# Splitting and reordering the VectorE, ScalarE and GpSimd steps of a seven-stage transformer kernel in full precision

## The chip, the cores and the metric

One core of a Trainium2 chip runs one kernel. The metric is device time in microseconds (us), the median of repeated executions. The engines are PE (TensorE, matmuls), DVE (VectorE), ACT (ScalarE), POOL (GpSimd) and SP (SyncE, which issues weight DMAs). Each has its own instruction stream and runs it in order; semaphores order the engines among each other.

## The reference, cut to what matters

Two blocks are computed on 512 tokens of width 1024, in float32 accuracy.

```python
# first_block, DEPTH = 2
for layer in range(2):
    f = swiglu(rms_norm(h, g[0]), gate[layer, 0], up[layer, 0], down[layer, 0]); h = h + 0.5 * rms_norm(f, g[1])
    hm = rms_norm(h, g[2])
    mix = pool_mixer(hm, ...) if layer == 0 else dilated_mixer(hm, cos, sin, w_q, k_sh, v_sh, w_o)
    h = h + rms_norm(mix, g[3])
    f = swiglu(rms_norm(h, g[4]), gate[layer, 1], up[layer, 1], down[layer, 1]); h = h + 0.5 * rms_norm(f, g[5])
# pool_mixer: u = hm @ w_in; p = causal means over 2, 4, 8, 16 tokens (one width per group of 256) - u;
#             ((p @ w_group) * scale) @ w_out
# dilated_mixer: rope(q), rope(k), three dilated windows, 8 heads of 64 each; softmax over the windows' log sums; @ w_o
# second_block, 2 layers, with 256 context tokens beside the 512
h = x * (1 + scale) + shift
q, k, v, gates ... = split(h @ w_in)          # also for the context tokens
y = [hgrn2 scan both ways, dense attention with rope, differential attention with rope, window attention with sink]
x = layer_norm(alpha * x + gate * ((y * silu(g)) @ w_out))
```

## The kernel before

Activations are kept feature-major: `hc` holds 8 blocks (`KC`) of 128 features by up to 768 tokens (`TOK`, 512 and 256 of context). Float32 accuracy comes from splitting each operand in two parts of fewer bits and making three matmuls per block: high x high, low x high and high x low (`mm3`, L1320). A weight tile is 128 by 1024. It is loaded by SP into `raw` (four slots); ACT copies it to its high part `wh` (L944), POOL subtracts to get the low part `wl` (L843, L855), and then PE may use it. The low part of the activations, `xl` or `al`, comes from DVE (`x_low`, L1973) or POOL (L893, L910).

The stages follow each other: a feed-forward (ffn) of layer 0 (0 to 395 us), the pool mixer (395 to 635, into which the next ffn's start falls), two ffns (the second, ffn(1,0), from 935), dilated attention (1335 to 1735), the fourth ffn (to 2131), and then the two layers of the second block (2131 to 2945 and 2945 to 3630), here called the last two layers. At each boundary `add_f` (L1977) normalizes the stage's result on DVE, adds it to `hc` block by block and makes the next stage's `xl`.

**Pool.** `POOL_TILES` (L48) is the order of ten weight tiles: eight "in" tiles, each followed by the means on DVE (L2114 to L2128), a high copy on ACT (L1058) and a low part on POOL (L910); and two "group" tiles on PE (L1495), which use PSUM banks 4 to 7.

**Rope tables.** `rope_tables` (L2142) computes angles on DVE at the start of ffn(1,0), and ACT makes two sines of them (L1027), in the same stream in which it copies `wh`.

**Dilated attention.** `dilated_steps` (L282) writes the order of PE, DVE and ACT: q, k and v tiles are computed in four quarters, after which "finish" adds a rotation matmul on PE (L1546), and at given quarters an "event" computes a unit of scores (L1560 the scores, L1566 the mask). DVE prepares rotated q and k (L2170, L2186). `kv_low` (L2220) makes the low parts of the normalized input of k and v. The output projection (L1641) begins when all low parts of the attention result are there (L1938), and DVE takes two PSUM banks at a time.

**The last two layers.** `mixer_steps` (L380) writes one list of steps per layer. Each engine walks through the same list and does its own share of every step, so the list sets the order within each engine. The steps are:

- `quarter` (a quarter of a 24-matmul weight tile on PE; with part 3, ACT's `wh` and gating of a tile and POOL's `wl`), `finish` (after a tile: rotations and splits on DVE, L2395 to L2444), `table` (ACT's DMA of a rope table);
- `scores` and `exps` of an attention (scores by query rows, whose maximum and sum give the softmax's row constants; ACT L1227), `rows` (DVE and ACT math of these constants, L2487 to L2513, transposed by PE, L1799, and copied by ACT, L1241);
- `weights` (scores again, by key, PE L1788, L1815; exponents by ACT L1250), `values` (PE L1836, L1846, L1879), `end` (normalization on DVE);
- steps of the two-way scan, the "ticks" of `scan_ticks`: `sums` in three stages (DVE L2308 to L2344, ACT L1154 the closing exponent), `dist` (POOL L876), `products` (PE L1681 to L1686, DVE L2267 to L2289), `step` (PE L1698 to L1709), `update` (L2304).

The waits between the engines are semaphores on each of these results.

## Time and profile before

| | us |
|---|---|
| median of 3 runs | 3629.45 (3626.37 to 3630.61) |
| profiled execution, own time | 3632.27 |
| span of that execution | 3630.3 |
| last two layers (2131 to 3630.3) | 1499.3 |

The span is the time between the first and the last instruction. Busy times of one engine are sums of its instructions; they can overlap those of the other engines, and matmuls overlap their neighbours on PE. The figure that says most is the idle time in front of an instruction and the work that ended it: "PE ps L1799 <- DVE work L2513" is PE at line 1799 waiting for what line 2513 wrote. "issue" says that no work of another engine ended the idle time. PEclk is the clock that TensorE was granted, 1.00 being 2.4 GHz.

### The profile page before, as it was taken

How to read it: one execution, taken by the hardware profiler on the slowest of the kernel's cores; microseconds unless marked ns; L12 is line 12 of the kernel's file. 1: busy time of each engine (PE TensorE's matmuls, PEld its weight loads, DVE VectorE, ACT ScalarE, POOL GpSimd, SP SyncE). 2: the span in 40 equal slices, each digit the busy share in tenths (PEclk: the TensorE clock that was granted, in tenths of full speed). 3: DMA queues.
4: the chain of work that ended last, by engine and by line, in shares of the span. 5: the costliest groups of instructions: out<-in, count | busy, mean ns of one | idle time of the engine just before them, and what ended most of it. 6: DMA issues, size and time to landing. Idle time of an engine off the chain costs nothing.

```text
span 3630.3 us, 53848 instructions
## 1 busy us (share of the span) xinstructions
PE 3244.4 (89%) x20644; PEld 2434.3 (67%) x20644; DVE 1747.4 (48%) x3135; ACT 1146.8 (32%) x1963; POOL 1216.3 (34%) x998
## 2 busy tenths in 40 slices
PE   7999889999899998998899988788979878688787
PEld 5888668777678776776678766555756655455454
DVE  4343765334634364444524366553653266554534
ACT  3222333212422132112312233443434234444343
POOL 3444444444344432222344444311331233213211
PEclk9999999999999999999999989988989988898889
DMA  3222222433233321111233321000101111001011
GB/s 134 93 98 97 77 82 82 139 122 110 100 126 107 133 81 64 53 59 47 81 133 110 122 105 36 25 19 24 36 14 64 47 53 36 30 25 36 24 53 41
DMA packets 74356, 264.66 MB, mean 73 GB/s; under 512 B 7856, under 2 KB 9136, under 8 KB 73904
## 3 DMA queue, kind: packets, MB, share of 16 engines
q1 hardware_dynamic: 67104, 242.25, 19.4%
q10 hardware_dynamic: 7056, 19.69, 1.5%
q8 instruction: 137, 2.24, 0.3%
q14 instruction: 59, 0.48, 0.0%
HBM read 252.47 MB, written 7.34 MB: 72 GB/s over the span
## 4 chain that ended last, share of the span: by engine, by line
PE 71%; DVE 15%; issue 7%; ACT 4%; POOL 2%; DMA 0%; ACTq 0%; DVEq 0%; POOLq 0%
PE ps L1320 53%; PE ps L1815 2%; PE ps L1836 2%; PE ps L1788 2%; POOL wl L855 1%; PE ps L1398 1%; DVE work L2071 1%; DVE tb L2473 1%; PE ps L1681 1%; DVE tb L2118 1%; PE ps L1623 1%; PE ps L1379 1%; PE ps L1641 1%; DVE hc L1984 1%; PE ps L1701 1%
## 5 line engine op out<-in xcount | busy, mean ns | idle before, releaser
L855 POOL TENSOR_TENSOR wl<-raw,wh 128x1024 fp32r<-128x1024 f32 x320 | 791.8, 2474 | 1220.6 <-ACT wh L966 705.4
L1320 PE MATMUL ps<-xh,wh 128*128 128x512 f32 x2400 | 916.2, 406 | 97.5 <-POOL wl L843 30.9
L1320 PE MATMUL ps<-xl,wh 128*128 128x512 f32 x2400 | 864.5, 385 | 0.0
L1320 PE MATMUL ps<-xh,wl 128*128 128x512 f32 x2400 | 862.8, 384 | 0.0
L1320 PEld LDWEIGHTS ps<-xh,wh 128*128 128x128 f32 x2400 | 442.8, 196 | 277.9 <-issue 155.5
L966 ACT ACTIVATE wh<-raw 128x1024 fp32r<-128x1024 f32 x224 | 237.6, 1061 | 982.4 <-PE ps L1320 934.0
L843 POOL TENSOR_TENSOR wl<-raw,wh 128x1024 fp32r<-128x1024 f32 x90 | 220.3, 2448 | 918.0 <-ACT wh L944 918.0
L1320 PEld LDWEIGHTS ps<-xl,wh 128*128 128x128 f32 x2400 | 443.1, 196 | 93.3 <-issue 13.1
L1320 PEld LDWEIGHTS ps<-xh,wl 128*128 128x128 f32 x2400 | 441.2, 195 | 87.6
L1320 PE MATMUL ps<-ah,wh 128*128 128x512 f32 x1104 | 437.5, 403 | 25.4 <-issue 14.2
L1320 PE MATMUL ps<-al,wh 128*128 128x512 f32 x1104 | 420.5, 388 | 0.0
L1320 PE MATMUL ps<-ah,wl 128*128 128x512 f32 x1104 | 420.3, 388 | 0.0
L944 ACT ACTIVATE wh<-raw 128x1024 fp32r<-128x1024 f32 x186 | 196.4, 1057 | 546.9 <-PE ps L1320 496.7
L1227 ACT ACTIVATE tb<-tb,work 128x256 f32<-128x256 f32 (+2 forms) x288 | 165.8, 576 | 385.0 <-DVE work L2479 185.8
L1320 PEld LDWEIGHTS ps<-ah,wh 128*128 128x128 f32 x1104 | 205.6, 189 | 106.6 <-issue 51.2
L2473 DVE TENSOR_SCALAR_CACHE_REDUCE tb<-ps 128x256 f32<-128x256 f32 (+2 forms) x288 | 135.3, 518 | 262.1 <-PE ps L1788 192.8
L2071 DVE TENSOR_TENSOR work<-work 128x512 f32<-128x512 f32 x88 | 245.2, 2786 | 0.0
L1320 PEld LDWEIGHTS ps<-ah,wl 128*128 128x128 f32 x1104 | 205.4, 189 | 43.1
L1320 PEld LDWEIGHTS ps<-al,wh 128*128 128x128 f32 x1104 | 206.0, 190 | 40.2 <-issue 2.0
L2067 DVE TENSOR_TENSOR work<-ps,rs 128x512 f32<-128x512 f32 x66 | 45.7, 692 | 300.2 <-PE ps L1320 300.1
L876 POOL TENSOR_TENSOR hc<-hc 128x64 f32<-128x64 f32 x280 | 95.7, 342 | 169.2 <-PE ps L1686 145.1
L1836 PE MATMUL ps<-work 128*64 128x512 f32 (+2 forms) x448 | 124.3, 636 | 21.0 <-issue 14.1
(348 smaller groups left out, 3625.3 us busy)
## 6 DMA issues: line engine op xcount, KB each, us to landing
raw<-wts_dram SPq DMA_DIRECT2D x458, 512.0 KB, 3.4
spilled_dram<-hc ACTq DMA_DIRECT2D x1, 3072.0 KB, 8.7
hc<-spilled_dram ACTq DMA_DIRECT2D x1, 3072.0 KB, 12.8
tb<-tab_dram ACTq DMA_DIRECT2D x5, 512.0 KB, 3.7
hc<-x_dram ACTq DMA_DIRECT2D x8, 256.0 KB, 9.2
spilled_dram<-hc ACTq DMA_DIRECT2D x1, 2048.0 KB, 7.2
hc<-spilled_dram ACTq DMA_DIRECT2D x1, 2048.0 KB, 9.3
out_dram<-hc SPq DMA_DIRECT2D x8, 256.0 KB, 2.1
```

What stands on the lines that cost most here:

```text
L843: pool.tensor_tensor(wl[:, n % SPLIT, :], raw[:, LOADED[n] % RAW, :], wh[:, n % SPLIT, :].bitcast(F32), ALU.subtract).then_inc(lo_done, 1)
L855: pool.tensor_tensor(wl[:, n % SPLIT, :], raw[:, LOADED[n] % RAW, :], wh[:, n % SPLIT, :].bitcast(F32), ALU.subtract).then_inc(lo_done, 1)
L876: pool.tensor_tensor(z[way], border, k_, ALU.subtract)
L944: act.activation(wh[:, n % SPLIT, :], raw[:, at % RAW, :], ACT.Copy).then_inc(hi_done, 1)
L966: act.activation(wh[:, n % SPLIT, :], raw[:, at % RAW, :], ACT.Copy).then_inc(hi_done, 1)
L1227: ins = act.activation(b, b, ACT.Exp, bias=m[:, lane, t:t + 1], scale=scale, accum_out=d[:, lane, t:t + 1])
L1320: ins = pe.matmul(out_, w[:, s, k * P:(k + 1) * P], x_(k, at), start=first, stop=last)
L1788: ins = pe.matmul(ps[:, score_bank(a) + lane, col_:col_ + n], x_[r0:r0 + w, q_tile * P:(q_tile + 1) * P], y_[r0:r0 + w, tok:tok + n], star ...
L1815: ins = pe.matmul(outs[lane], stat, mov, start=number == 0, stop=number == 3 and not g["masks"], skip_group_check=True)
L1836: pe.matmul(flat[HEAD * h:HEAD * (h + 1), g["q0"]:g["q0"] + g["n"]], vv, pring[t % len(pring)][:, 0:g["n"]], start=g["first"], stop=g["las ...
L2071: dve.tensor_tensor(tt[:, j, :], tt[:, j, :], sil[:, j, :], ALU.mult).then_inc(dve_own, 1)
L2473: ins = dve.tensor_scalar(scores_copy[:, lane, col_:col_ + n], ps[:, score_bank(a) + lane, col_:col_ + n], 1.0, -3e38, ALU.mult, ALU.max, ...
```

## The change

1. `add_f`: `xl` of block k-1 is made before the addition of block k, not after it.
2. Pool: the group-2 tile moves behind the last two in tiles; the two groups get banks of their own (`group_bank`, `pool_bank`), so that PE waits for fewer PSUM banks to come free (the second group no longer waits for the first one's four low parts, and the output tiles run in other banks); POOL makes the `wl` of the next tile before the `al` of the tile ahead.
3. `rope_tables` on DVE moves from the start of ffn(1,0) to the start of ffn(0,1), in buffers that are free there. ACT's sines stay.
4. Dilated: the scores' event of a v tile moves from quarter 1 to quarter 2, so that two products of three matmuls stand between the rotation and the scores that need it; `kv_low` is spread in three pieces; the output projection begins with three of four blocks before it waits for the last low part, and DVE takes one bank at a time.
5. `mixer_steps`: ACT's and POOL's share of a finished tile becomes a step of its own, "round", which is put off behind the next `weights` (`later`); the second half of a rotation becomes "rope"; the row constants' math becomes "math", directly behind the last scores, and "rows" comes after the last `values`; "square" (ACT, differential attention) comes right behind the last `values`; "y", the split of a mixed result, moves from `end` of one attention to behind the first `values` of the next; DVE's wait for the rope table ("table_in") moves from the DMA's issue to before its first use; the scan's `sums` get up to six stages and extra ticks; a unit of scores is put in directly behind `values` where two or more are due.

In the diff, "..." marks what is left out.

```diff
-POOL_TILES = [("in", 6), ("in", 7), ("in", 4), ("in", 5), ("in", 2), ("in", 3), ("group", 2), ("in", 0), ("in", 1), ("group", 0)]
+POOL_TILES = [("in", 6), ("in", 7), ("in", 4), ("in", 5), ("in", 2), ("in", 3), ("in", 0), ("in", 1), ("group", 2), ("group", 0)]
...
+        if part == 3 or part == 1 and what != "v" or part == 2 and what == "v":
             event()
...
-        ticks += [[("sums", w, stage)] for stage in range(3)]
+        long = [["scan"], ["rest", "keys"]] if way else [["scan", "keys"]]
+        stages = [["abs"], ["logs"], *([["more"]] if layer else []), *long, ["exp"]]
+        ticks += [[("sums", w, stage) for stage in together] for together in stages]
+        ticks[-2].append(("dist", w, 0))
...
-    steps, ends, ticks = [], [], []
+    steps, ends, ropes, rounds, maths, ticks = [], [], [], [], [], []
 
     def scores(a, u):
+        if u == 0:
+            flush(ropes)
         steps.extend([("scores", a, u), ("exps", a, u)])
-
-    def quarter(f, part):
-        while f[0] == "g" and f[1] in SCANS and part == 3 and ("sums", 4 * layer + 2 * SCANS.index(f[1]) + 1, 0) not in steps:
+        if a and u == units[a] - 1:
+            maths.append(("math", a))
...
+    def flush(what):
+        steps.extend(what)
+        what.clear()
+
+    def quarter(f, part, later=False):
...
+        if part == 3:
+            flush(ropes)
+            flush(rounds)
+            if f in (("q", 2), ("q", 4)):
+                steps.append(("table_in",))
         steps.append(("quarter", f, part))
+        if part == 3:
+            rounds.append(("round", f))
+            if not later:
+                flush(rounds)
         if part == 3 and (f[1] not in SCANS and f[0] not in "gm" or f[0] == "i"):
             ends.append(("finish", f))
         if part == 3 and f in (("f", "s0"), ("f", "s1")):
             ticks.extend(scan_ticks(layer, SCANS.index(f[1])))
 
     def finishes():
-        steps.extend(ends)
+        if ends:
+            flush(rounds)
+        for _, f in ends:
+            steps.append(("finish", f))
+            if f[0] in "qk":
+                ropes.append(("rope", f))
         ends.clear()
...
+    def extra_tick():
+        if ticks and ticks[0][0][0] == "sums":
+            tick()
...
+            if i == 0:
+                finishes()
             if i + 1 < n:
                 steps.append(("weights", a, i + 1))
+            flush(rounds)
             finishes()
+            flush(maths)
             if i == n - 1 and not last:
                 for q in fill[i]:
                     quarter(*q)
                 finishes()
-                steps.append(("rows", a + 1))
                 fill[i] = []
             steps.append(("values", a, i))
+            if i == n - 1:
+                steps.append(("square", a))
+            if i == 0 and a:
+                steps.append(("y", a - 1))
+            extra_tick()
+            if len(due[i]) > 1:
+                scores(a + 1, due[i].pop(0))
             between = [None] if len(fill[i]) < 2 else [fill[i].pop(0), None]
             between += [*fill[i][:1], None, *fill[i][1:]]
             for number, step in enumerate(between):
                 if step:
-                    quarter(*step)
+                    quarter(*step, later=True)
                 else:
+                    flush(maths)
                     tick()
+                    flush(ropes)
                 if number % 2 == 0 and due[i]:
                     scores(a + 1, due[i].pop(0))
             for u in due[i]:
                 scores(a + 1, u)
+        flush(ropes)
+        if not last:
+            steps.append(("rows", a + 1))
         if a in (1, 3):
             finishes()
             tick(len(ticks))
+        quarter(*tail, later=True)
         if not last:
             steps.append(("weights", a + 1, 0))
-        quarter(*tail)
+        flush(rounds)
         steps.append(("end", a))
         if a == 3:
             steps.append(("reload",))
     finishes()
+    steps.append(("y", len(ATTENDS) - 1))
...
+        def group_bank(g0, b):
+            return (4 if g0 else 0) + b
+
+        def pool_bank(m):
+            return (m + 4) % 8
...
-                    elif step == "quarter" and at[1] == 3:
+                    elif step == "round":
                         remainder(c.at("tile"))
                         c.take("tile")
...
+                    late = []
                     for what, m in POOL_TILES:
                         remainder(c.at("tile"))
                         c.take("tile")
-                        if what == "in":
+                        for k in late:
                             pool.wait_ge(part_hi, c.take("part") + 1)
-                            pool.tensor_tensor(alk(m), tt[:, m % 2, :], ahk(m).bitcast(F32), ALU.subtract).then_inc(a_ready, 1)
-                        else:
-                            c.take("part", 4)
+                            pool.tensor_tensor(alk(k), tt[:, k % 2, :], ahk(k).bitcast(F32), ALU.subtract).then_inc(a_ready, 1)
+                        late = [m] if what == "in" else []
+                    c.take("part", 8)
...
-                wait_a(A_HEADS // 2)
+                wait_a(A_HEADS // 2 - 1)
                 settle()
+                c.take("a")
...
-                    ins.then_inc(tile_done, 1)
+                    for b, k in [(b, k) for k in range(4) for b in range(2)] if m == 0 else [(b, k) for b in range(2) for k in range(4)]:
+                        if (m, b, k) == (0, 0, 3):
+                            pe.wait_ge(a_ready, c.at("a"))
+                        blk = b * 4 + k
+                        for w, x_, first, last in ((wh, ah, k == 0, False), (wh, al, False, False), (wl, ah, False, k == 3)):
+                            ins = pe.matmul(ps[:, bb[b], :], w[:, n % SPLIT, blk * P:(blk + 1) * P],
+                                            x_[:, (KC + k) * SEQ:(KC + k + 1) * SEQ], start=first, stop=last)
+                        if k == 3:
+                            ins.then_inc(tile_done if b else half_full, 1)
...
                     own(dve.scalar_tensor_tensor(t, fo[:, k, :], gain(k), r, ALU.mult, ALU.mult))
+                    if k and name != "ada":
+                        x_low(k - 1, gain_of(name, *at))
                     give(dve.tensor_tensor(hc[:, k, 0:SEQ], hc[:, k, 0:SEQ], t, ALU.add), h_ready, "h")
                     if name == "ada":
                         modulated(at[0], k)
-                    elif k:
-                        x_low(k - 1, gain_of(name, *at))
...
-                ang, u, v = (fo[:, k, :] for k in range(3))
-                own(dve.tensor_copy(fo[:, 3, :], t1[:, 1, :].bitcast(I32)))
-                own(dve.tensor_scalar(ang, fo[:, 3, :], const("invf"), None, ALU.mult))
+                u, ang = t1[:, 0, :], t1[:, 1, :]
+                own(dve.tensor_copy(u, t1[:, 1, :].bitcast(I32)))
+                own(dve.tensor_scalar(ang, u, const("invf"), None, ALU.mult))
...
-                    give(dve.tensor_scalar(fo[:, 4 + s, :], v, PI_IN, -PI_IN, ALU.min, ALU.max), d2a, "d2a")
+                    give(dve.tensor_scalar(v, v, PI_IN, -PI_IN, ALU.min, ALU.max), d2a, "d2a")
...
                     if step == "quarter" and at[1] == 3:
                         take(*at[0])
                         if at[0] == DILATED_TILES[1]:
-                            kv_low()
+                            kv_low(0, 1, 2)
+                        if at[0] == DILATED_TILES[2]:
+                            kv_low(5, 6, 7)
                     elif step == "finish":
                         finish(*at)
+                        if at[0] == DILATED_TILES[1]:
+                            kv_low(3, 4)
...
                     if m:
-                        add_square(m - 2), add_square(m - 1)
+                        add_square(m - 1)
+                    b = 2 * (c.at("tile") % 2)
+                    dve.wait_ge(half_full, m // 2 + 1)
+                    dve.tensor_copy(fo[:, m, :], ps[:, b, :]).then_inc(half_taken, 1)
+                    dve.wait_ge(half_taken, m // 2 + 1)
+                    add_square(m)
                     n = tile()
-                    b = 2 * (n % 2)
-                    took(dve.tensor_copy(fo[:, m:m + 2, :], ps[:, b:b + 2, :]), n)
-                add_square(KC - 2), add_square(KC - 1)
+                    took(dve.tensor_copy(fo[:, m + 1, :], ps[:, b + 1, :]), n)
+                add_square(KC - 1)
                 add_f(norm_gain(1, 3), "ffn", 1, 1)
```

How the rows move on the engines, at three places:

PE, dilated attention, first k tile with a unit of scores (L1546/L1609 is the rotation, L1560/L1623 the scores, L1320/L1385 quarters of the v tile). Before:

```order
L1546 MATMUL ps<-work,cn 128x512
L1560 MATMUL ps<-work 128x128 x8
L1566 MATMUL ps<-mk 128x128 x8
L1320 MATMUL ps<-ah,wh 128x512
L1320 MATMUL ps<-al,wh 128x512
```

Changed:

```order
L1609 MATMUL ps<-work,cn 128x512
L1385 MATMUL ps<-ah,wh 128x512
L1385 MATMUL ps<-al,wh 128x512
L1385 MATMUL ps<-ah,wl 128x512
L1385 MATMUL ps<-ah,wh 128x512
L1385 MATMUL ps<-al,wh 128x512
L1385 MATMUL ps<-ah,wl 128x512
L1623 MATMUL ps<-work 128x128 x8
L1629 MATMUL ps<-mk 128x128 x8
```

Six matmuls now stand between the rotation and the scores.

DVE, layer 0 of the last two, around the row constants of the third attention (L2440 to L2444 is the end of a rotation, L2495 to L2513 the row constants; L2523 to L2527 and L2578 to L2596 in the changed kernel). Before:

```order
L2341 MEMSET work 128x256
L2342 MEMSET hc 128x128
L2440 TENSOR_TENSOR work<-work,tb 128x512
L2441 TENSOR_TENSOR work<-work 128x512
L2442 CAST ex<-work 128x512
L2444 TENSOR_TENSOR ex<-work,ex 128x512
L2495 TENSOR_TENSOR work<-work 128x16
L2502 TENSOR_TENSOR work<-work 128x16
```

Changed:

```order
L2556 TENSOR_SCALAR tb,work<-ps 128x256 x4
L2570 TENSOR_SCALAR work<-work 128x2x2
L2578 TENSOR_TENSOR work<-work 128x16
L2585 TENSOR_TENSOR work<-work 128x16
L2586 TENSOR_TENSOR work<-work 128x16
L2590 TENSOR_TENSOR work<-work 128x24
```

The row constants follow their last scores (L2556, L2570), and the rotation comes behind them.

ACT, the last layer, at the scan's sums (L1154/L1214 is their closing exponent, L1250/L1311 the exponents of the attention weights, L944/L1008 a `wh`, L1218/L1276 the rope table). Before:

```order
L1227 ACTIVATE tb,work<-tb,work 128x256 x4
L989 ACTIVATE hc<-hc 128x768
L990 ACTIVATE hc<-hc,sm 128x768
L1218 DMA tb<-tab_dram 128x1024
L1154 ACTIVATE work<-work,sm 128x768
L1250 ACTIVATE work<-ps 128x512 x2
```

Changed:

```order
L1285 ACTIVATE tb,work<-tb,work 128x256 x4
L1053 ACTIVATE hc<-hc 128x768
L1054 ACTIVATE hc<-hc,sm 128x768
L1276 DMA tb<-tab_dram 128x1024
L1311 ACTIVATE work<-ps 128x512 x2
L1008 ACTIVATE wh<-raw 128x1024
```

The weights' exponents and a `wh` no longer stand behind the closing exponent of the sums.

## Rows read from the trace of the kernel before

**Rows 1.** The page, part 1: busy us (share of the span) xinstructions

```profile
PE 3244.4 (89%) x20644; PEld 2434.3 (67%) x20644; DVE 1747.4 (48%) x3135; ACT 1146.8 (32%) x1963; POOL 1216.3 (34%) x998
```

**Rows 2.** Busy time by stretch: its length, PE, PEld, DVE, ACT, POOL busy, PEclk, DMA, GB/s

```profile
395.00:635.00 240.00, 216.14 (x863) 165.77 (x862) 149.25 (x161) 80.53 (x108) 97.46 (x43) 0.96 0.22 76
1335.00:1735.00 400.00, 362.56 (x2162) 270.58 (x2161) 183.22 (x224) 85.58 (x116) 99.44 (x40) 0.96 0.16 54
2131.00:2945.00 814.00, 677.10 (x6554) 486.51 (x6555) 422.30 (x1164) 315.61 (x695) 211.85 (x385) 0.90 0.10 36
2945.00:3630.30 685.30, 550.93 (x4588) 366.71 (x4588) 360.68 (x948) 279.23 (x597) 170.74 (x269) 0.87 0.11 38
```

**Rows 3.** PE's waits, 2131 to 3630.3: us in total, times, longest us

```profile
PE ps L1788 <- ACT work L1250: 39.2, 13, 15.7
PE ps L1799 <- DVE work L2513: 30.8, 10, 8.8
...
PE ps L1698 <- DVE work L2289: 24.0, 17, 6.9
...
PE ps L1815 <- issue: 17.6, 9, 4.9
...
PE ps L1815 <- ACT work L1250: 9.9, 5, 5.4
...
PE ps L1846 <- ACT work L1258: 8.9, 4, 3.3
```

**Rows 4.** Boundary: PE's waits 0 to 2131, and the timeline of DVE (start, us)

```profile
PE ps L1320 <- DVE xl L1975: 24.5, 5, 5.3
...
537.23 0.69 DVE L1984 TENSOR_TENSOR hc<-hc,work 128x512 f32<-128x512 f32 x1
```

**Rows 5.** Pool stage: PE's waits 395 to 635, then timelines of DVE and POOL

```profile
PE ps L1320 <- POOL wl L843: 6.1, 5, 2.9
PE ps L1495 <- POOL al L910: 4.3, 1, 4.3
...
473.53 0.67 DVE L2125 SCALAR_TENSOR_TENSOR work<-tb 128x496 f32<-128x496 f32 x1
...
477.25 2.72 DVE L2125 SCALAR_TENSOR_TENSOR work<-tb 128x496 f32<-128x496 f32 x1
...
475.37 1.30 POOL L910 TENSOR_TENSOR al<-work,ah 128x512 fp32r<-128x512 f32 x1 [2.42 <-ACT ah L1058]
476.64 2.81 POOL L843 TENSOR_TENSOR wl<-raw,wh 128x1024 fp32r<-128x1024 f32 x1
```

**Rows 6.** Rope tables: timelines of DVE, ACT and PE; DVE at ffn(0,1)'s start

```profile
949.53 0.42 DVE L2146 CAST work<-tb 128x512 f32<-128x512 int32 x1
...
959.03 0.63 ACT L1027 ACTIVATE tb<-work 128x512 f32<-128x512 f32 x1 [3.39 <-DVE work L2156]
...
963.07 0.80 PE L1320 MATMUL ps<-xh,wh 128*128 128x512 f32 x1 [7.07 <-POOL wl L855]
...
558.29 0.69 DVE L2065 TENSOR_TENSOR work<-ps,rs 128x512 f32<-128x512 f32 x1 [5.80 <-ACT rs L982]
```

**Rows 7.** Dilated attention: PE's waits, 1335 to 1735; one third of the output projection's matmuls

```profile
PE ps L1560 <- DVE work L2186: 11.1, 6, 1.9
PE ps L1546 <- DVE work L2170: 6.8, 5, 4.2
...
PE ps L1641 <- DVE al L1938: 4.0, 1, 4.0
...
L1641 PE MATMUL ps<-ah,wh x32: 388/389/796, 1701.8 to 1725.8; 128*128 128x512 f32 x32
```

**Rows 8.** Last layer: timelines of DVE and of ACT

```profile
3112.77 0.96 DVE L2325 SCALAR_TENSOR_TENSOR hc<-hc 128x768 f32<-128x768 f32 x1 [4.59 <-DMA tb<-tab_dram]
...
3120.26 0.93 ACT L1154 ACTIVATE work<-work,sm 128x768 f32<-128x768 f32 x1 [10.24 <-DVEq L2344]
```

**Rows 9.** POOL's waits, 2131 to 3630.3

```profile
POOL wl L843 <- ACT wh L944: 869.4, 74, 37.6
```

132 lines of the change are left out of this document (73 added, 59 removed).

## Prediction

> **What bounds the kernel now.** I read the page's first part, then busy time by stretch, then PE's waits, and last the timelines around the longest of them. PE is busy 89% of the span and no other engine is above half [rows 1], so what counts is PE's idle time and the clock PE is granted. In the last two layers PE is busy 677.1 of 814.0 us and 550.9 of 685.3 [rows 2]: 136.9 + 134.4 = 271.3 us idle, most of the kernel's idle 386 us (3630.3 - 3244.4). The granted clock there is 0.90 and 0.87, against 0.96 in the pool and dilated stages [rows 2]; at most 0.10 x 677.1 + 0.13 x 550.9 = 139 us of busy time is there because the clock was low. Two things can be won: idle time, and with it some of these 139 us, since PE's lower clock goes with the stretches that have more idle time. DVE is busy 52% of the time in these layers [rows 2], so it is no bound by volume; PE waits for it because of the order of its instructions.
>
> **The change, part by part.** Each term is a gain against the profiled execution, 3632.27 us, which stands 2.8 above the median of the runs.
>
> *Boundaries.* PE's first matmul of a stage waits for `xl`, 24.5 us in 5 places [rows 4]. At each, the addition of the next block, 0.69 us [rows 4], moves behind the `xl` that PE waits for. 5 x 0.69 = 3.5; I take **3**. Bounds: 1 (the last `xl` sets the end and nothing is won elsewhere) and 4.
>
> *Pool.* The removable waits are 6.1 us for `wl` in five places, and 4.3 for the `al` before the first group tile [rows 5]. With both group tiles last, that `al` is older, and `wl` ahead of `al` helps the first wait. Against it: the `wl` took 2.81 us directly behind an `al` of 1.30 [rows 5]; now this pair always runs as a block of 4.1 us, in which a DVE operation of 0.67 us took 2.72 [rows 5], and DVE sets the period of the means. I take half of 10.4, **5**, bounds -2 (2.72 - 0.67 once more than now) and 8. That a DVE operation on two SBUF inputs slows down beside POOL is stated in the Trainium skill, GPSIMD Engine Reference, in the table at its top: the SBUF interfaces are shared with VectorE. By that rule alone the amount of slowed work would stay, whichever of `wl` and `al` goes first, and this term would be nearly 0 instead of 5. The trace agrees with the rule in kind (0.67 against 2.72 us).
>
> *Rope tables.* PE stands 7.07 us at the first down tile of ffn(1,0) [rows 6]: ACT's second sine waits for DVE (3.39) and the `wh` for which POOL's `wl` is needed stands behind it. With the angles made one ffn earlier the sines wait for nothing: **about 8.5** (7.07 and some slow clock after it). But 9.5 us of DVE work, from its first row at 949.53 to the second sine at 959.03, now stand in front of the first multiplication of ffn(0,1), where DVE idles 5.80 us waiting for ACT's reciprocal root [rows 6]. The 3.7 us above that can make PE wait once; I charge 2.5. Net **6**, bounds 0 (the whole 7 returns there) and 8.
>
> *Dilated attention.* PE waits 11.1 us at the scores (6 long ones, up to 1.9) and 6.8 at rotations, 4.2 of it behind `kv_low`'s eight in a row; 4.0 before the output projection [rows 7]. The 96 matmuls of the output projection, in three groups of 32 like the one shown, take 24.5 us from first to last start [rows 7], 0.25 each; six are 1.5 us of cover for six waits of 1.85 in the mean: 9, and 1 of the other waits at rotations. Five of eight `kv_low` leave the spot: 3. Eighteen matmuls (4.6 us) before the last low part: 3. One bank instead of two as the last copy: 2. That is 18 of the 37.4 us idle in this stretch; its low clock costs at most 0.04 x 362.6 = 14.5, and 18/37.4 of that is 7. Together **25**. Bounds: 12 (half of the waits only move on, since DVE has the same work) and 35.
>
> *The last two layers, idle time.* By class [rows 3]:
> - L1788 behind ACT L1250, 39.2 in 13, one of 15.7: ACT's closing exponent of the scan sums waited 10.24 us for DVE, which itself waited 4.59 for the rope table [rows 8], and the weights' exponents queued behind it. The new order has these exponents ahead of the closing one: 15. The other 23.5: 10, from scores issued sooner and rounds (1.04 us of `wh`) put behind exponents.
> - L1799 behind the row constants L2513, 30.8 in 10: the math moves up before the rotation, and the last `values` lie between it and the transposes: 22; 9 is left, where DVE is late anyhow.
> - L1815, 17.6 and 9.9: PE at the weights with nothing or ACT to wait for: 12, as `wh` and gating no longer precede its exponents.
> - L1846 behind the square, 8.9: the square is now issued right after `values`: 6.
> - L1698 behind the scan's DVE chain, 24.0 in 17: 5, since DVE has as much to do as before.
>
> That is 70. What is put off has to be waited for somewhere: 55 rounds, the rope multiplications and "y". I charge 10. Net **60** of 271.3.
>
> *The clock.* 60/271.3 x 139 = 31; since 139 is an upper bound (the mean counts idle stretches too), **22**. Bounds for the two together: 25 (only the 15.7 and the squares go, 5 of clock) and 160 (39.2 + 30.8 + 17.6 + 9.9 + 8.9 = 106 idle, and 106/271.3 of 139, 54, for the clock).
>
> Where I could go wrong in reading rows 2 as work: the Trainium skill, Perfetto Trace Analysis (Identifying the Most-Contended Engine), holds that matmul busy time is a bad measure and the busy share of weight loads a better one. Here that is 486.5/814 = 60% and 366.7/685.3 = 54%, against PE's 83% and 80% [rows 2]. By it more than my 271 us could be won in these layers; the sum goes by idle time and clock.
>
> Sum: 3 + 5 + 6 + 25 + 60 + 22 = 121. 3632.3 - 121 = 3511; less 2.8 for the median (3508.5): **3508 us**.
>
> **The rivals.**
>
> *A, waits only move.* DVE has the same instructions in the last two layers (12 more rows in all); its chain (L1698) becomes what PE waits for next. Against it: DVE idles half the time. Then the last two layers give 25 and the other parts half of their terms or less, 1 + 1 + 2 + 15: 44, and the time is 3632 - 44 - 3 = 3585.
>
> *B, the clock comes back.* If a PE that idles less keeps 2.4 GHz in most stretches, clock and idle time give 80 + 60 instead of 82: 3632 - 39 - 140 - 3 = 3450. For it: with idle shares of 10 and 9% the pool and dilated stretches have 0.96, with 17 and 20% the last layers 0.90 and 0.87 [rows 2].
>
> *C, slower: late weights.* 55 of 76 rounds are put off behind weights' exponents. A round is 1.04 us of `wh` on ACT and then 2.4 to 2.8 of `wl` on POOL, 3.5 in all. If the tile's low part is late by this every time, PE stands 55 x 3.5 = 192 us and the time is 3508 + 192 = 3700. It decides from 121/55 = 2.2 us per round on. Against it: POOL waits for `wh` 869.4 us in 74 places, 11.7 each [rows 9], so `wl` is not short of POOL's time, and no wait of PE for L843 is among those of rows 3, whose view goes down to some 4 us. What the rows don't show is how early the tile is ready; that is why C keeps a chance.
>
> *D, the change does nothing measurable*: its steps are ordered otherwise but each wait is ended by the same data, 3629. The long waits of rows 3 and 8 are waits for order, not data, so this is unlikely.
>
> **How the numbers follow.** Forecast 0.66 (3470 to 3555), A 0.17, B 0.10, C 0.04, D 0.03. The range 3450 to 3590 holds the forecast, A's 3585 and B's 3450, and leaves out C, D and the ends beyond. A measurement of this kernel can tell about 0.2% (7 us) from no change. Faster by more than that: 0.66 + 0.17 + 0.10 = 0.93; same 0.03; slower 0.04.
>
> **What would show it.** Right: PE's wait at the first down tile of ffn(1,0) under 2 us; the scores' waits in dilated attention under 0.6 each; no wait above 10 us in the last two layers; L1799's successor waiting for DVE at most 10 us in all; idle there near 211 instead of 271 us, with PEclk 0.91 to 0.93 in the higher of the two. Wrong: PE waits for `wl` (L843's successor) in the last two layers (C); waits for DVE chains growing by what the others lost (A); PEclk unchanged while idle falls, which would make the clock term 0 and the time 3530.

## The result, and the profile after

The changed kernel takes **3580.5 us** (median of 4 runs, 3576.4 to 3584.2); the kernel before took 3627.9 beside it. The ratio is 0.9867, 95% interval 0.9848 to 0.9885: 47 us gained where 121 were forecast. The profiled execution has a span of 3582.3 us, 48.0 less than the 3630.3 of before. The page's first part, after:

```profile
PE 3239.6 (90%) x20644; PEld 2428.5 (68%) x20644; DVE 1748.5 (49%) x3139; ACT 1142.8 (32%) x1963; POOL 1209.8 (34%) x998
```

Each stage begins with a matmul that waits for `xl`, so its start can be read in both traces to 0.01 us. From one such start to the next (the last to the end):

| from ... to | before | after | gained | forecast |
|---|---|---|---|---|
| pool, to ffn(0,1) | 133.6 | 132.3 | 1.3 | 5 |
| ffn(0,1) and ffn(1,0) | 801.0 | 806.2 | -5.1 | 6 |
| dilated, to ffn(1,1) | 399.1 | 374.3 | 24.8 | 25 |
| ffn(0,0) and ffn(1,1) | 804.1 | 804.2 | 0.0 | - |
| first of the last two layers | 807.2 | 790.1 | 17.1 | |
| second of them | 685.3 | 675.3 | 10.0 | 82 for both |

(The differences are taken before rounding. The 3 us of the boundaries lie within these stages.) Busy time by stretch, dilated and the last two layers, cut at those starts; columns as in [rows 2]. Before:

```profile
1339.89:1738.99 399.10, 361.94 (x2156) 270.05 (x2157) 183.03 (x224) 85.58 (x117) 99.44 (x40) 0.96 0.16 55
2137.83:2945.02 807.19, 676.73 (x6552) 486.22 (x6553) 416.31 (x1152) 314.31 (x693) 210.05 (x384) 0.91 0.10 36
2945.02:3630.30 685.28, 550.93 (x4588) 366.69 (x4588) 360.66 (x948) 279.23 (x597) 170.74 (x269) 0.87 0.11 38
```

After:

```profile
1343.72:1718.01 374.29, 355.43 (x2157) 262.59 (x2157) 182.41 (x228) 85.32 (x116) 99.34 (x40) 0.99 0.16 58
2116.93:2907.04 790.11, 670.31 (x6552) 482.43 (x6553) 422.35 (x1152) 312.72 (x693) 204.66 (x384) 0.91 0.10 37
2907.04:3582.30 675.26, 552.42 (x4588) 368.75 (x4588) 353.60 (x948) 277.93 (x597) 166.51 (x269) 0.87 0.11 38
```

In dilated attention idle time fell from 37.2 to 18.9 us and busy time by 6.5, with the clock at 0.99 instead of 0.96. In the last two layers idle time fell only from 264.8 to 242.6 us, busy time by 5, and the clock stayed at 0.91 and 0.87. PE's waits there after, from the same view as [rows 3]:

```profile
PE ps L1764 <- DVE work L2366: 45.0, 31, 7.4
PE ps L1385 <- issue: 28.4, 17, 6.2
...
PE ps L1747 <- DVE hc L2347: 21.0, 10, 8.6
PE ps L1881 <- issue: 18.5, 7, 6.6
PE ps L1829 <- DVEq L2609: 18.2, 6, 4.4
PE ps L1835 <- ACT work L1229: 16.1, 2, 11.2
PE ps L1854 <- ACT work L1311: 10.8, 17, 2.7
...
PE ps L1865 <- DVE work L2596: 3.6, 2, 2.5
```

Most of the waits that I had aimed at went: the weights behind ACT (L1788, now L1854) from 39.2 us to 10.8, the transposes behind the row constants (L1799, now L1865) from 30.8 to 3.6, the 8.9 behind the square altogether. Others grew: the scan's step (L1698, now L1764) from 24.0 in 17 places [rows 3] to 45.0 in 31; the scan's products (L1681, now L1747) from 11.8 to 21.0; L1763, now L1829, from 8.6 to 18.2, in four of its six places (16.1 us) behind the `end` of a differential attention; 16.1 at the norm (L1835), of which one is 11.2. Two of them before:

```profile
PE ps L1681 <- DVE hc L2270: 11.8, 11, 2.2
...
PE ps L1763 <- DVEq L2526: 8.6, 6, 2.0
```

### The profile page after: what moved, and what is told of

It reads as the page before. It is cut to its first block, busy times and chain, and to the rows that moved or that the text cites. A ratio compares the mean times of both kernels' runs of the same rounds, so it can differ in the third digit from the quotient of the medians.

```text
span 3582.3 us, 53865 instructions
## 1 busy us (share of the span) xinstructions
PE 3239.6 (90%) x20644; PEld 2428.5 (68%) x20644; DVE 1748.5 (49%) x3139; ACT 1142.8 (32%) x1963; POOL 1209.8 (34%) x998
## 4 chain that ended last, share of the span: by engine, by line
PE 68%; DVE 16%; issue 9%; ACT 4%; POOL 2%; DMA 0%; ACTq 0%; DVEq 0%; POOLq 0%; SPq 0%
PE ps L1385 51%; PE ps L1881 2%; PE ps L1904 2%; PE ps L1854 2%; POOL wl L918 2%; DVE tb L2556 1%; ACT tb L1285 1%; DVE work L2139 1%; PE ps L1747 1%; PE ps L1686 1%; DVE work L2359 1%; PE ps L1444 1%; PE ps L1767 1%; DVE hc L2054 1%; DVE work L2362 1%
## 5 line engine op out<-in xcount | busy, mean ns | idle before, releaser
L918 POOL TENSOR_TENSOR wl<-raw,wh 128x1024 fp32r<-128x1024 f32 x320 | 792.8, 2478 | 1201.4 <-ACT wh L1030 705.6
L1385 PE MATMUL ps<-xh,wh 128*128 128x512 f32 x2400 | 913.1, 405 | 97.1 <-POOL wl L906 31.2
L1385 PE MATMUL ps<-xl,wh 128*128 128x512 f32 x2400 | 860.8, 383 | 0.0
L1385 PE MATMUL ps<-xh,wl 128*128 128x512 f32 x2400 | 859.0, 382 | 0.0
L1385 PEld LDWEIGHTS ps<-xh,wh 128*128 128x128 f32 x2400 | 442.7, 196 | 261.2 <-issue 139.5
L1385 PEld LDWEIGHTS ps<-xl,wh 128*128 128x128 f32 x2400 | 440.9, 195 | 93.3 <-issue 13.2
L1385 PEld LDWEIGHTS ps<-xh,wl 128*128 128x128 f32 x2400 | 437.7, 193 | 87.6
L1385 PE MATMUL ps<-ah,wh 128*128 128x512 f32 x1104 | 441.2, 407 | 29.0 <-issue 17.4
L1385 PE MATMUL ps<-al,wh 128*128 128x512 f32 x1104 | 420.5, 388 | 0.0
L1385 PE MATMUL ps<-ah,wl 128*128 128x512 f32 x1104 | 420.3, 388 | 0.0
L1008 ACT ACTIVATE wh<-raw 128x1024 fp32r<-128x1024 f32 x186 | 196.3, 1057 | 453.2 <-PE ps L1385 424.0
L1385 PEld LDWEIGHTS ps<-ah,wh 128*128 128x128 f32 x1104 | 205.2, 189 | 112.4 <-issue 55.6
L2556 DVE TENSOR_SCALAR_CACHE_REDUCE tb<-ps 128x256 f32<-128x256 f32 (+2 forms) x288 | 135.2, 517 | 242.6 <-PE ps L1854 169.3
L2139 DVE TENSOR_TENSOR work<-work 128x512 f32<-128x512 f32 x88 | 245.3, 2787 | 0.0
L1385 PEld LDWEIGHTS ps<-ah,wl 128*128 128x128 f32 x1104 | 205.2, 189 | 43.6
L1385 PEld LDWEIGHTS ps<-al,wh 128*128 128x128 f32 x1104 | 205.7, 189 | 42.2 <-issue 4.3
L1311 ACT ACTIVATE work<-ps 128x512 f32<-128x512 f32 (+2 forms) x224 | 108.6, 536 | 208.8 <-PE ps L1881 164.1
## 6 DMA issues: line engine op xcount, KB each, us to landing
hc<-spilled_dram ACTq DMA_DIRECT2D x1, 3072.0 KB, 10.5
```

Of the source, the lines that this page charges most:

```text
L918: pool.tensor_tensor(wl[:, n % SPLIT, :], raw[:, LOADED[n] % RAW, :], wh[:, n % SPLIT, :].bitcast(F32), ALU.subtract).then_inc(lo_done, 1)
L1008: act.activation(wh[:, n % SPLIT, :], raw[:, at % RAW, :], ACT.Copy).then_inc(hi_done, 1)
L1311: act.activation(pring[t % len(pring)][:, 0:g["n"]], ps[:, weight_bank(a, i, lane), 0:g["n"]], ACT.Exp, scale=scale).then_inc(exp_done, 1)
L1385: ins = pe.matmul(out_, w[:, s, k * P:(k + 1) * P], x_(k, at), start=first, stop=last)
L2139: dve.tensor_tensor(tt[:, j, :], tt[:, j, :], sil[:, j, :], ALU.mult).then_inc(dve_own, 1)
L2556: ins = dve.tensor_scalar(scores_copy[:, lane, col_:col_ + n], ps[:, score_bank(a) + lane, col_:col_ + n], 1.0, -3e38, ALU.mult, ALU.max, ...
```

## The experiments

Times of a stage are read as above, from one profile each. Four profiles hold the same part 5 (the changed kernel twice, p5 and rope_back): 1465.4, 1455.1, 1458.7 and 1460.9 us for the last two layers, mean 1460. The spread of 10 us lies in PE's busy time (1213.6 to 1222.7); its idle time is 239.8 to 242.6, so it repeats within 3 us. A difference below 10 us between the stages of two single profiles is therefore shown only where the idle time moves with it by more than 3 us, or where the runs of the whole kernels on one chip lie apart. A table of all runs stands at the end of this section. Ratios are to the kernel before on the same chip.

### Which part gave what

p14 is the kernel before with parts 1 to 4 of the change (of the diff ahead, `POOL_TILES`, the events of `dilated_steps`, the POOL, PE and DVE pieces of the pool and dilated stages, `add_f` and `rope_tables`), p5 the one with part 5 alone (`scan_ticks`, `mixer_steps` and the engines' shares of its new steps).

> Parts 1 to 4 alone (boundaries, pool, rope tables, dilated), the last two layers as before. Theory 'by the trace': the first matmul of the last two layers came 20.9 us earlier in the changed kernel (24.8 gained in dilated attention, 5 lost by the rope tables, about 1 gained by boundaries and pool), and parts 1 to 4 touch nothing behind it: 3628 - 21 = 3607, with the same waits in the last two layers as before. Rival 'the prediction's terms': 39 us gained, 3589. Rival 'coupled': the earlier stages change what the clock grants later, then the last two layers differ from 1492 us (2137.8 to 3630.3) by over 5.

> Part 5 alone (the last two layers' order), the first stages as before. Theory 'by the trace': from their first matmul to the end the last two layers took 1492.5 us before and 1465.4 changed, so 27 us: 3628 - 27 = 3601. Rival 'the prediction's term': 82 us, 3546. If p14 and this one don't sum to the 47 us of the whole, the parts are coupled.

p14: ratio 0.9937 (0.9916 to 0.9958), last two layers 1492.8 us against 1492.5 before, dilated 373.6. p5: 0.9903 (0.9872 to 0.9935), last two layers 1458.7. The two add up to 1.6% against 1.33% for the whole, which the intervals allow. No coupling of the parts shows, and both were overestimated in the prediction.

The changed kernel once more, without an edit:

> The changed kernel itself, on the chip of the other two, to see how far a stage's time moves between chips and profiles: last two layers 1465.4 us in its first profile, 1458.7 and 1460.9 in the two runs that have the same part 5. Theory: 1458 to 1466, ratio to before 0.9867 within 0.002.

Ratio 0.9852 (0.9836 to 0.9869), last two layers 783.1 + 671.9 = 1455.0: 3 us below the interval that I had given from three profiles, so one kernel's time in these layers moves by up to 10 us.

### The rope tables

```diff
-                if (layer, i) == (0, 1):
+                if (layer, i) == (1, 0):
                     rope_tables()
```

> The changed kernel with the rope angles computed at the start of ffn(1,0) again, in the new buffers. Theory 'the cover was short': the 9.5 us of DVE work in ffn(0,1) cost PE 5.8 us and some 3 us of half clock there, and saved 7.1 and as much half clock; the wait of 5.8 at the first down tile of ffn(0,1) goes, one of about 7 at ffn(1,0) comes back, and ffn(0,1)+ffn(1,0) become 3 to 6 us shorter in the trace: 3576. Rival 'the move is worth the 6 us that I summed': 3587.

Ratio 0.9835 (0.9810 to 0.9861). ffn(0,1) and ffn(1,0) together: 801.8 us, against 802.3 to 806.2 in the ten profiles with the angles at the start of ffn(0,1) (mean 803.3), and 801.0 before and in p5. So the 6 us that I had are not there, and the move rather costs 1 to 3; the ratios alone can't tell this. The two halves are clear: ffn(0,1) is 395.7 us without it (397.1 before) and 405 to 407 with it, ffn(1,0) 406.1 (403.9 before) against 397 to 399. How it costs the first of them, in the changed kernel (timelines of DVE, POOL and PE):

```profile
552.83 0.42 DVE L2214 CAST tb<-tb 128x512 f32<-128x512 int32 x1
...
555.28 2.85 POOL L918 TENSOR_TENSOR wl<-raw,wh 128x1024 fp32r<-128x1024 f32 x1 [21.64 <-ACT wh L1008]
555.92 2.76 DVE L2221 SCALAR_TENSOR_TENSOR tb<-tb 128x512 f32<-128x512 f32 x1
...
564.56 0.69 DVE L2133 TENSOR_TENSOR work<-ps,rs 128x512 f32<-128x512 f32 x1 [0.22 <-DVE tb L2225]
...
569.70 0.80 PE L1385 MATMUL ps<-xh,wh 128*128 128x512 f32 x1 [5.78 <-POOL wl L918]
```

The chain starts at 552.83 and the first multiplication comes at 564.56, 6.3 us later than before [rows 6], and 7.6 later counted from the stage's first matmul, not 3.7: an operation of 0.69 us took 2.76 beside POOL. ACT's second `wh` and POOL's `wl` follow it, and PE stands 5.78 us.

### The math of the row constants

```diff
         steps.extend([("scores", a, u), ("exps", a, u)])
-        if a and u == units[a] - 1:
-            maths.append(("math", a))
...
                 finishes()
+                steps.append(("math", a + 1))
                 fill[i] = []
```

> The changed kernel with the row constants' math back at its old place, before the last values' predecessors, and the transposes ('rows') at their new place. Theory 'DVE waits for ACT': math directly behind the last scores makes DVE wait up to 4 us for ACT's exponents, with the scan's products queued behind it; without it PE's waits for the scan (45.0 us at L1764, 21.0 at L1747) fall by 15 or more and the time is about 3568. Rival 'early math is a gain': the transposes wait for late math again, L1865's 3.6 us grow by over 10, and the time is 3590.

Ratio 0.9792 (0.9766 to 0.9817): faster than the change as made. The last two layers take 787.7 + 658.7 = 1446.4 us, 14 below the mean of the four, all of it in the second layer. PE's waits in math_old:

```profile
PE ps L1763 <- DVE work L2365: 39.8, 32, 7.4
...
PE ps L1384 <- issue: 20.9, 18, 2.5
PE ps L1746 <- DVE hc L2346: 20.2, 9, 8.6
...
PE ps L1864 <- DVE work L2595: 7.0, 3, 3.9
```

The scan's waits fell from 66.0 to 60.0 us, not by 15, and the waits at quarters of tiles behind "issue" from 28.4 to 20.9; the transposes wait 3.4 more. Against the mean of the four, idle time fell by 8.5 us and busy time by 5. DVE's own waits for ACT within the math fell only from 21 to 16 us in these layers. The size was as expected; that DVE's waits for ACT are the cause is shown only in part. Both kernels still have a chain like the one that the theory describes, at the first attention. In the changed kernel's last layer (timelines of DVE and PE):

```profile
3007.82 0.75 DVE L2511 SCALAR_TENSOR_TENSOR work<-work,pr,ps 128x512 f32<-128x512 f32 x1 [3.96 <-ACT ps L1236]
...
3010.07 0.17 DVE L2578 TENSOR_TENSOR work<-work 128x8 f32<-128x8 f32 x1
...
3012.42 0.17 DVE L2596 TENSOR_TENSOR work<-work,hcol 128x8 f32<-128x8 f32 x1
...
3013.31 1.03 DVE L2347 TENSOR_TENSOR hc<-hc,work 128x64 f32<-128x64 f32 x7
...
3014.39 0.36 PE L1747 MATMUL ps<-work 64*32 64x32 f32 x16 [8.56 <-DVE hc L2347]
```

DVE first idles 3.96 us for ACT, but ahead of the last step of a norm (L2511) and not of the math; then the math takes from 3010.07 to 3012.42, going twice to ACT and back, and the scan's operands (L2347) and PE stand behind both. What becomes of it when this math is moved back is tried in best2 below.

```diff
                 finishes()
                 steps.append(("math", a + 1))
+                steps.append(("rows", a + 1))
...
-        if not last:
-            steps.append(("rows", a + 1))
```

> math_old with the transposes of the row constants ('rows': PE, and ACT's copy) back ahead of the last values as well, so that only the math/rows split is undone altogether. Theory 'the last values cover the chain': PE waits 8.8, 6.4, 4.6 and 4.2 us again at the transposes (L1864's wait grows from 7.0 to about 30 us) and the last two layers take 15 to 25 us more than math_old's 1446. Rival 'the wait only moved behind the values': within 3 us of it.

Ratio 0.9853 (0.9828 to 0.9878), last two layers 797.9 + 664.0 = 1461.9 us: 15.5 more than math_old (idle time 8.3, busy time 7.2). So the transposes behind the last `values` are a real gain, at the low end of what I expected. Their waits grew by 8.6 us, to 15.6 and not to 30; a new wait of 8.1 stands at the norm of the differential attention (L1912), and other waits fell:

```profile
PE ps L1863 <- DVE work L2594: 15.6, 6, 4.5
...
PE ps L1912 <- DVE work L2475: 8.1, 1, 8.1
```

### The extra ticks

```diff
             tick()
-        else:
-            extra_tick()
```

> math_old without the extra tick in the opening part of each of the last two layers (where the first attention's tiles are made). Theory 'DVE's queue': a stage of the scan's sums (more, scan and keys, 6 us of DVE) stood ahead of the copy of the q tile, so PE waited 4.9 and 11.2 us at the norm's matmul (L1834) and 8.6 at the scan's products; without it both layers' L1834 waits fall to below 6 in all (5.4 + 0.9 before the change), and the last layer gets 5 to 10 us shorter than math_old's 658.7. Rival 'the sums are needed then': their later place makes the scan's products or gates wait by as much, and the layers stay within 3 us of math_old's 787.7 and 658.7.

Ratio 0.9760 (0.9727 to 0.9793), last two layers 774.5 + 655.2 = 1429.7 us, 16.7 less than math_old. The norm's waits fell from 16.1 to 6.2 us. Of the 16.7, idle time gave 7.2. Most of the gain is in the first layer (13.2, busy time 6.9 of it), where PE had waited only 4.9 us; the last layer got 3.5 us shorter and not 5 to 10. So the norm's waits went as expected, and the rest of the gain is unexplained. What the extra tick did, in the changed kernel (DVE, ACT, PE):

```profile
2958.75 1.02 DVE L2416 SCALAR_TENSOR_TENSOR hc<-hc,sm,work 128x768 f32<-128x768 f32 x1
...
2960.56 0.69 DVE L2483 COPY work<-ps 128x512 f32<-128x512 f32 x1
...
2961.34 0.63 ACT L1229 ACTIVATE work<-work 128x512 f32<-128x512 f32 x1 [5.70 <-DVEq L2484]
...
2962.12 1.19 PE L1835 MATMUL ps<-work,cn 128*128 128x512 f32 x1 [11.23 <-ACT work L1229]
```

The sums (L2416 and the 4 us before it) stand ahead of the copy of the q tile (L2483), with ACT's square of it behind that, and PE waits 11.23 us.

```diff
     def extra_tick():
-        if ticks and ticks[0][0][0] == "sums":
-            tick()
+        pass
```

> math_old with no extra tick anywhere, so that all stages of the sums come at the old rate. Theory 'DVE's queue': the waits of 6.2 and 3.2 us in layer 0 and 4.1 in the last at the weights (L1880 behind 'issue', DVE's rest and keys stages ahead of the scores) go too, another 5 us less than m_nopro. Rival: the scan then ends later (its stages are six instead of three) and the last tick(len(ticks)) of each attention pair piles up steps: waits at L1763 and L1746 grow by over 10 us and the time is above math_old's.

Ratio 0.9718 (0.9684 to 0.9753), last two layers 766.7 + 658.3 = 1425.0 us: 4.7 less than m_nopro, as expected. Idle time fell by 8.1, and the runs on this chip lie apart (3527.7 to 3542.9 us against 3544.2 to 3556.5). Its waits:

```profile
PE ps L1762 <- DVE work L2364: 27.3, 18, 7.4
PE ps L1745 <- DVE hc L2345: 26.5, 14, 8.5
...
PE ps L1879 <- issue: 10.2, 4, 3.2
...
PE ps L1833 <- ACT work L1227: 6.3, 2, 5.4
```

Against math_old the step's waits came down from 39.8 to 27.3, the weights' from 19.5 to 10.2, while the products' grew from 20.2 to 26.5.

### The steps put off

```diff
-                ropes.append(("rope", f))
+                steps.append(("rope", f))
```

> math_old with the second half of a rotation ('rope') directly behind its 'finish' again. Theory 'every put-off step only moves a wait': the time stays within 3 us of math_old's, because rope (2.5 us of DVE) stands ahead of scores' maxima instead of behind them. Rival 'putting off rope is a real gain': L1853 and L1763 waits grow by 10 us or more.

Ratio 0.9811 (0.9780 to 0.9841), last two layers 1456.0 us, 9.6 more than math_old, idle time 5.9 of it: the put-off rotation is a gain, though the intervals of the two ratios overlap. The wait is at weights behind DVE's scores (9.3 us in 5 places) and at the products (6.1 more). My theory, that every put-off step only moves a wait, falls here.

```diff
-            if not later:
-                flush(rounds)
+            flush(rounds)
```

> math_old with no round put off (ACT's wh and gating, POOL's wl at once after the tile). Theory 'rounds behind the exponents are the real gain of part 5': the waits for weights' exponents (L1853 <- ACT L1310, 10.5 us now, 39.2 + 9.9 before the change) return by 15 us or more, and the last two layers take about 1465 instead of 1446 us. Rival 'they cost nothing either way': within 3 us.

Ratio 0.9773 (0.9743 to 0.9804), last two layers 1439.6 us, 6.8 *less*, but not by its waits: idle time is 3.9 us more, busy time 10.7 less, and busy time alone moves by 9 between profiles of the same code. The waits for the weights' exponents did return (10.5 to 25.7 us), and most of it went elsewhere (the weights behind "issue" from 19.5 to 9.7). Neither the expected 15 us nor a gain is shown.

```diff
-            if i == 0 and a:
-                steps.append(("y", a - 1))
...
         steps.append(("end", a))
+        steps.append(("y", a))
```

> math_old with 'y' (DVE's split of a mixed result, some 1.5 us) directly behind 'end' again. Theory 'DVE's queue': the exponents' weights and the next scores wait behind it once per attention, 6 per layer, up to 1.5 us each: 5 to 10 us slower than math_old. Rival 'no one waits there': within 3 us.

Ratio 0.9803 (0.9782 to 0.9824), 1442.8 us: within 4 of math_old, idle time within 1. No one waits there for long enough to show.

### A version that beats both, and two doubts

best1 is math_old without extra ticks and without put-off rounds (both edits above), and with the rope angles in the middle of ffn(0,1):

```diff
-                if (layer, i) == (0, 1):
-                    rope_tables()
...
                     dve.wait_ge(a_ready, a0 + part)
+                    if (layer, i, number) == (0, 1, 1):
+                        rope_tables()
                     if number < len(FF_PARTS) - 1:
```

> math_old, no extra ticks, no round put off, and the rope angles in the middle of ffn(0,1), behind the gates of its second part and ahead of its down tiles. By the sums of the single runs: last two layers 1446.4 - 21.4 - 6.8 = 1418; rope: ffn(0,1) and ffn(1,0) 396 + 398 = 794 us instead of 802 to 806, because DVE idles there; in all 3582 - 47 - 10 = 3525. Rival 'the gains overlap': no_later's and no_extra's gains are the same waits (ACT's and DVE's queue at the first scores), then 1425 and 3532.

Ratio **0.9716** (0.9693 to 0.9739), 3528.4 us: 104 us less than before on that chip, twice the gain of the change. ffn(0,1) and ffn(1,0): 396.0 + 399.0 = 795.0 us as forecast, 6.0 less than before, 1.0 of it by the boundaries; four kernels with the angles there have 795.0 to 797.3. The chain was not shorter there: 14.0 us in one piece (777.67 to 791.71), with two operations of 2.76 and 2.60 us beside POOL. But PE went on with the down tiles meanwhile, and DVE caught up on them afterwards. The last two layers:

```profile
2105.25:2868.05 762.80, 664.13 (x6553) 481.18 (x6553) 415.88 (x1152) 315.64 (x693) 208.18 (x384) 0.92 0.11 38
2868.05:3525.60 657.55, 538.32 (x4588) 361.75 (x4588) 360.31 (x948) 280.04 (x597) 168.62 (x269) 0.89 0.12 39
```

1420.4 us, of which 217.9 idle. Against before, idle time fell by 47 us and busy time by 25 (1227.7 to 1202.5). 1418 and 1425 had been forecast; single profiles can't tell these two apart.

```diff
-        if number == 0:
-            steps.append(("math", 0))
...
+    steps.append(("math", 0))
     steps.append(("rows", 0))
```

> best1 with the first attention's row constants' math directly ahead of its transposes instead of one quarter earlier. Theory 'DVE waits for ACT's exponents': the 8.5 us wait at the scan's products in the last layer (L1745) and 7.4 at its step in layer 0 fall by half, 8 us less than best1. Rival: the transposes then wait for the math: same time within 3 us.

Ratio 0.9749 (0.9729 to 0.9768), 1430.1 us: 9.8 more, idle time 3.8 of it; the runs on this chip lie apart (3539.6 to 3544.1 us against 3525.5 to 3535.6). The two long waits fell by 2.5 us each, to 6.1 and 4.9, and not by half, and the time rose. The theory falls for the first attention. The waits at the products and at the transposes, first in best1, then in best2:

```profile
PE ps L1744 <- DVE hc L2344: 33.1, 13, 8.6
...
PE ps L1862 <- DVE work L2593: 7.1, 4, 3.5
```

```profile
PE ps L1743 <- DVE hc L2343: 28.0, 15, 6.1
...
PE ps L1861 <- DVE work L2592: 16.8, 6, 5.0
```

5 us go at the products and 10 come at the transposes.

```diff
-        stages = [["abs"], ["logs"], *([["more"]] if layer else []), *long, ["exp"]]
+        stages = [["abs"], ["logs"], [*(["more"] if layer else []), *[s for t in long for s in t], "exp"]]
...
-        ticks[-2].append(("dist", w, 0))
...
-            ticks.append((here("dist", p) if p else []) + here("products", p - 2) + here("take", p - 2) + here("decay", p - 1))
+            ticks.append(here("dist", p) + here("products", p - 2) + here("take", p - 2) + here("decay", p - 1))
```

> best1 with the scan's sums in three stages as before (more, scan, rest, keys and exp in one tick), dist 0 with the first decay again. Theory 'finer stages are a gain once they come at the old rate': DVE is blocked for up to 8 us again, with weights' exponents behind the closing exponent, and waits such as the 15.7 us one return: 15 us or more slower than best1's 1420 in the last two layers. Rival 'the split of the sums was worth nothing': within 4 us.

Ratio 0.9839 (0.9823 to 0.9855), last two layers 784.2 + 678.9 = 1463.1 us, **43 more** than best1 (idle time 27, busy time 15). The finer stages of the sums, with the first `dist` that moved along with them, are the largest gain found in part 5; how much of it is `dist` alone was not tried. The long wait is back, in the same place (ACT, then PE):

```profile
3066.17 0.93 ACT L1210 ACTIVATE work<-work,sm 128x768 f32<-128x768 f32 x1 [7.51 <-DVEq L2418]
...
3068.12 0.79 PE L1850 MATMUL ps<-ah,ex 64*128 64x512 f32 x2 [13.17 <-ACT work L1307]
```

> best1 with rounds put off behind the next weights' exponents again. Theory 'the put-off rounds cost': 7 us slower, as between m_nolater and math_old. Rival 'the 7 us came with the extra ticks': within 3 us.

(`if not later` back in best1.) Ratio 0.9730 (0.9714 to 0.9746), 1418.3 us, within 3 of best1: once the extra ticks are gone it makes no difference whether rounds are put off. The idle times agree too (217.2 and 217.9).

PE's time in the last two layers, from one profile each (us; added up before rounding):

| run | idle | busy | both |
|---|---|---|---|
| before | 264.8 | 1227.7 | 1492.5 |
| p14 | 263.5 | 1229.2 | 1492.8 |
| changed | 242.6 | 1222.7 | 1465.4 |
| changed again | 241.5 | 1213.6 | 1455.1 |
| p5 | 241.6 | 1217.2 | 1458.7 |
| rope_back | 239.8 | 1221.1 | 1460.9 |
| math_old | 232.9 | 1213.5 | 1446.4 |
| rows_old | 241.2 | 1220.7 | 1461.9 |
| m_nopro | 225.7 | 1203.9 | 1429.6 |
| m_noextra | 217.6 | 1207.4 | 1425.0 |
| m_ropenow | 238.8 | 1217.2 | 1456.0 |
| m_nolater | 236.8 | 1202.8 | 1439.6 |
| y_old | 233.4 | 1209.4 | 1442.8 |
| best1 | 217.9 | 1202.5 | 1420.4 |
| best2 | 221.7 | 1208.3 | 1430.1 |
| b_scan3 | 245.3 | 1217.8 | 1463.1 |
| b_later | 217.2 | 1201.1 | 1418.3 |

## Why the prediction was wrong, by its own steps

- **Boundaries, 3.** Right: the five waits for `xl` went from 5.3, 5.3, 4.3, 4.3 and 5.3 us to 5.0, 4.6, 3.6, 4.0 and 4.6, 2.7 in all.
- **Pool, 5.** Mis-sized: about 1. The waits for `wl` didn't fall, the `al` fell by 0.8 (4.3 to 3.5; [rows 5] before):

```profile
PE ps L1385 <- POOL wl L906: 6.5, 5, 2.6
PE ps L1385 <- POOL wl L918: 6.2, 2, 5.8
PE ps L1559 <- POOL al L974: 3.5, 1, 3.5
```

  (The wait of 5.8 for L918 is the one in ffn(0,1) and belongs to the rope tables.) The slowed DVE work moved instead of going: of the eight operations of one line, one was slow before and four after. L2125, now L2193 (minimum, median, maximum in ns), before and after:

```profile
L2125 DVE SCALAR_TENSOR_TENSOR work<-tb x8: 674/675/2724, 428.8 to 477.3; 128x496 f32<-128x496 f32 x8
```

```profile
L2193 DVE SCALAR_TENSOR_TENSOR work<-tb x8: 675/1163/2734, 429.1 to 472.4; 128x496 f32<-128x496 f32 x8
```

  Other lines lost as much, so that DVE's busy time in the whole stage (its third figure of busy time) hardly moved, 89.87 us before and 91.18 after:

```profile
405.30:538.85 133.55, 115.59 (x452) 87.77 (x453) 89.87 (x100) 44.91 (x63) 55.66 (x26) 0.95 0.21 71
```

```profile
405.26:537.56 132.30, 116.18 (x453) 87.71 (x453) 91.18 (x100) 44.65 (x62) 57.89 (x26) 0.94 0.21 74
```

  The table at the top of the Trainium skill's GPSIMD Engine Reference (Specifications) says that GpSimd shares its SBUF interfaces with VectorE. I had read from it that order alone gives nearly 0. The measured 1 us is nearer to that than to the 5 us that I took from the waits.
- **Rope tables, 6.** Wrong in the step "the 3.7 us above that can make PE wait once; I charge 2.5". The chain took 11.7 us to the first multiplication and not 9.5, and PE lost 8 to 11 us in ffn(0,1) where I charged 2.5. The gain in ffn(1,0) was 5 to 9 by the kernel that it is compared with, so the 8.5 is not refuted. Put ahead of the down tiles, the same work cost PE nothing that shows (ffn(0,1) 396.0 in best1, 396.1 in p5 without it).
- **Dilated, 25.** Right in size, and nearly so in its items (24.8): idle time 18.3 less (18 forecast), busy time 6.5 less (7 forecast for the clock). The waits after:

```profile
PE ps L1609 <- DVE work L2239: 4.4, 5, 1.8
PE ps L1623 <- DVE work L2255: 2.9, 6, 0.6
...
PE ps L1653 <- ACT work L1148: 1.3, 1, 1.3
```

  11.1 at the scores became 2.9 (9 forecast), the rotations' 6.8 became 4.4 (4 forecast), the output projection's 4.0 went.
- **Last two layers, idle, 60.** Wrong: 22, and 23 in the mean of the four profiles. Of the classes listed, the weights behind ACT fell by 28 (25 forecast), the transposes by 27 (22) and the square by 8.9 (6); L1815, now L1881, where I had 12, did not (27.5 before, 18.5 + 5.7 and smaller ones after). The steps that failed are "5, since DVE has as much to do as before" and "I charge 10" for what is put off, and that the extra ticks had no term at all: the scan's waits (step and products) grew by some 30 us, from 35.8 to 66.0, the norm's by 9, L1829's by 10. By the experiments the change held gains and losses: finer sums (43, with no extra ticks), late transposes 15, put-off rotations 10, against extra ticks (21 on math_old) and early math of the later attentions (14 in the mean). I had counted early math as part of a gain. With both losses taken out and the rounds as before, best1 has the last two layers 72 us shorter, of the 82 forecast for idle time and clock; most of the gains that I summed were there, and the two losses hid them. The square shows in small how a wait moves on: its own (8.9) went, and the next one, for the `end` of the same attention, grew from 6.9 to 16.1 us in the four places.
- **The clock, 22.** 5 in the first profile, 9 in the mean of the four. It follows the idle time, which fell by 23 and not by 60: 9 for 23 is the share that I had taken (22 for 60), so the term failed with the idle time and not by itself. In best1 the relation was the full one, 25 us of busy time for 47 of idle time, where 139/271 of 47 is 24.
- **Rival A** had the mechanism (the scan's DVE chain is what PE waits for next) in part, and nearly the time, 3585; I gave it 0.17. Its 25 for the last two layers (27 measured) was a good estimate; that the whole came so near is partly luck, since it had 15 for dilated attention, where 24.8 came, and 2 gained by the rope tables, where some us were lost. Nor is it the whole cause: in best1 the scan's waits are still 58.3 us, as A has it, and yet 47 us of idle time are gone. C was not seen: `wl` is in none of the listed waits of the last two layers. Nor was B: the granted clock stayed as it was.
- **The signs.** Seen: the scores' waits (at most 0.6), the transposes (3.6), the first down tile of ffn(1,0) (1.4 instead of 7.1). Not seen: idle time is 242.6 and not 211, PEclk 0.91 in the higher of the two layers but 0.87 in the other, as before, and one wait is still above 10 us (11.2).

The evidence that I passed over is in [rows 3] itself: 17 waits for DVE's chain of the scan beside 13 for ACT. DVE's half share of busy time says that it has room in the mean, not at the places where its steps stand in front of what PE needs.

## What to carry to other kernels

The order of an in-order queue has to be priced step by step: what a step waits for, and what then stands behind it. Here a long step gained by being split (43 us), and lost when its pieces were then issued sooner (21 us). A chain that goes back and forth with another engine lost by being moved up for the later attentions (14 us), and lost by being moved back for the first one (10 us), so each place needs its own trial. Side work belongs where what stands behind it can wait: the rope angles cost PE nothing ahead of the down tiles, although they took 14 us there, and 8 to 11 us ahead of the first multiplication of a stage, where they took 11.7. And idle time, which repeats within 3 us here, tells more from one profile than the stage's whole time, which moves by 10.

## What was not expected of the hardware

DVE operations on two SBUF operands of 128x496 or 128x512 took up to 2.7 to 2.8 us instead of 0.7 beside a POOL subtraction, wherever they were put (2.72 and 2.76 above). One on a single operand was slow too: a `tensor_scalar` of the rope angles took 2.60 us instead of 0.43 in best1, beside a POOL subtraction that ran from 786.07 for 2.39 us. A chain planned next to POOL should be costed so. The busy time of PE fell with its idle time: 9 us for 23 in the last two layers (mean of the four profiles of the changed order), 25 for 47 in best1, 6.5 for 18.3 in dilated attention.
